# Output projection and routing inside the mixer's block, the front turned by scaled diagonals, token sums in four places

## What is computed

```python
h = rmsnorm(x, g_mix)
q, fg, inp, og, cb, cc, ch, ga, gb = split(h @ w_in)        # 9 slices of 1024 columns
o, s_new = hgrn2_scan(silu(q), (1 - lb) * sigmoid(-fg), inp, logf, s_hg)
o = rmsnorm(o, g_hg_out) * silu(og)
y_a = o @ w_br_a
conv = sum(ext[:, j:j + l] * w_conv[j] for j in range(3))   # ext: cc * ch behind its history
y_b = (cb * conv) @ w_br_b
x = x + (sigmoid(ga) * y_a + sigmoid(gb) * y_b) @ w_out
t = rmsnorm(x, g_ffn)
# top 1 of 4 groups, top 2 of its 8 experts, weights of the two normalised
x = x + hier_moe(t)
x = x + sigmoid(rmsnorm(x, g_ple) @ w_ple_gate) * (p @ w_ple_proj)
return rmsnorm(x, g_final)
```

## Time and profile before

| | |
|---|---|
| median of 3 runs | 1222.99 us (1220.28 to 1223.65) |
| profiled execution | 1231.61 us |
| its span, first to last instruction | 1229.8 us |
| PE busy | 1133.2 us, 92% |
| DVE busy | 641.3 us, 52% |
| POOL, ACT busy | 290.3 and 245.9 us |
| mean granted clock of TensorE | 0.957 |
| moved by DMA | 191.57 MB |

### The profile page before, as it was taken

How to read it: one execution, slowest core, us unless ns; L and a number is a source line. 1 busy time by engine, 2 the same in 40 slices (tenths; PEclk the granted TensorE clock), 3 DMA queues, 4 the chain that set the end, 5 groups by cost and what they waited for, 6 DMA issues and landing times. The chain is left out here.

```text
span 1229.8 us, 15391 instructions
## 1 busy us (share of the span) xinstructions
PE 1133.2 (92%) x5839; PEld 817.8 (67%) x5839; DVE 641.3 (52%) x1279; ACT 245.9 (20%) x446; POOL 290.3 (24%) x242
## 2 busy tenths in 40 slices
PE   4999999999999999899999998898599998887896
PEld 3888888788888877688888884446355554443442
DVE  6356777846477777545535453444234333332655
ACT  3142220104222111341111000111012211112221
POOL 2204221222331113244343440010132221121000
PEclk9999989999999899999999998897699999899998
DMA  6223211321512135222223417303699999997301
GB/s 222 70 71 105 69 35 55 109 86 35 172 39 69 37 108 177 76 70 90 82 69 103 147 49 300 163 35 151 227 386 390 376 383 397 396 399 289 122 34 39
DMA packets 96466, 191.57 MB, mean 156 GB/s; under 512 B 10454, under 2 KB 73766, under 8 KB 84104
## 3 DMA queue, kind: packets, MB, share of 16 engines
q1 hardware_dynamic: 90500, 181.21, 41.0%
q0 software_dynamic: 5440, 8.94, 2.3%
q10 hardware_dynamic: 452, 0.42, 0.1%
HBM read 180.17 MB, written 17.98 MB: 161 GB/s over the span
## 5 line engine op out<-in xcount | busy, mean ns | idle before, releaser
L1093 PE MATMUL ps<-arena,weights 128*128 128x272 f32 x2240 | 535.5, 399 | 6.5 <-DVE arena L765 3.4
L1093 PEld LDWEIGHTS ps<-arena,weights 128*128 128x128 f32 x2240 | 426.6, 192 | 99.5 <-issue 5.1
L583 POOL TENSOR_TENSOR weights<-weights 128x512 f32<-128x512 f32 x160 | 216.7, 1362 | 516.0 <-PE ps L1093 460.1
L1608 PE MATMUL ps<-arena 128*64 128x256 f32 x864 | 108.1, 407 | 16.0 <-DMA arena<-in_w_up 15.9
L1608 PEld LDWEIGHTS ps<-arena 128*64 128x64 f32 x864 | 63.7, 146 | 50.8 <-DMA arena<-in_w_up 17.6
L1686 DVE TENSOR_SCALAR arena<-arena 64x256 f32<-64x256 f32 x32 | 9.1, 286 | 140.5 <-ACT arena L1650 140.5
L1276 PE MATMUL ps<-weights,arena 128*128 128x512 f32 (+1 forms) x160 | 72.0, 653 | 4.2 <-PEq L483 4.2
L627 ACT ACTIVATE arena<-ps 128x272 f32<-128x272 f32 x80 | 31.1, 393 | 219.3 <-PE ps L1093 219.3
L1573 POOL DMA_INDIRECT expert_rows<-arena x32 | 29.3, 914 | 187.1 <-DVE arena L1702 182.1
L771 DVE TENSOR_TENSOR arena<-arena 128x272 f32<-128x272 f32 x40 | 39.8, 996 | 48.7 <-ACT arena L627 48.4
L1863 PE MATMUL ps<-arena 128*128 128x512 f32 (+1 forms) x160 | 63.0, 594 | 1.4 <-DVE arena L1932 1.4
(11 more groups left out here) (244 smaller groups left out, 1184.9 us busy)
## 6 DMA issues: line engine op xcount, KB each, us to landing
weights<-in_w_in SPq DMA_DIRECT2D x36, 1024.0 KB, 5.1
arena<-in_w_gate SPq DMA_DIRECT2D x27, 1024.0 KB, 21.9
arena<-in_w_up SPq DMA_DIRECT2D x27, 1024.0 KB, 28.4
arena<-in_w_down SPq DMA_DIRECT2D x27, 1024.0 KB, 30.5
weights<-in_w_gate SPq DMA_DIRECT2D x5, 1024.0 KB, 24.5
weights<-in_w_up SPq DMA_DIRECT2D x5, 1024.0 KB, 31.7
weights<-in_w_down SPq DMA_DIRECT2D x5, 1024.0 KB, 31.1
arena<-in_x_prompt SPq DMA_DIRECT2D x8, 512.0 KB, 6.2
```

The costliest lines, as they stand in the source:

```text
L583: nc.gpsimd.tensor_tensor(SW[:, i], x, y, op).then_inc(s_ready, 1)
L1093: ins = mm(ps[:, b, 0:HF], w4[:, k, :], x4[:, k, :], start=(k == 0), stop=(k == 3))
L1608: ins = mm(ps[u * UP:u * UP + CAP, 2 + s, 0:DE], xgT[s][:, k, :], w[e % 6][:, k, :], start=(k == 0), stop=(k == KT - 1))
```

## The change

There are four parts. (1) **Front**: x is no longer scaled. DVE multiplies the identity by a tile's root and gets a diagonal (`root_rows`), and PE multiplies the rows of x by the diagonal, which turns and scales at once. The short tile is loaded and squared third instead of fifth, conv history is copied later, POOL's first sums wait for all five diagonals, and the first mixer product waits for tiles 0 to 2. (2) **Token sums**: `cvout` stands after three products of the first gb pair instead of behind the pair, and the four subtractions of T1 stand one behind each og pair. (3) **Projection and routing** move into the mixer's block: the functions `out_sync`, `out_pool`, `out_tensor`, `out_scalar` and `out_vector` are called at the end of each engine's stream, the barrier is gone, and a semaphore `mix_ready`, raised behind each ya pair, stands in its place. (4) **Order** on PE, DVE and ACT in that stage: the projection is cut into quarters (512 columns, four K steps), with the turn, the logits and the rank products between them. The bodies of the moved functions are as before where the diff doesn't show them.

```diff
@@ schedule()
-        ev += [("sq", 2 * p), ("sq", 2 * p + 1), *pair("gb", p), *([] if p else [("cvout", 0), ("T", 1)]), ("stat", 2 * p), ...
-    ev += pairs("og", 0) + pairs("og", 1) + pairs("ga", 0) + pairs("ga", 1) + [("T", 2)] + ...
+        gb = pair("gb", p)
+        ev += [("sq", 2 * p), ("sq", 2 * p + 1), *gb[0:3], *([] if p else [("cvout", 0)]), *gb[3:], ("stat", 2 * p), ...
+    for p in range(4):
+        ev += pair("og", p) + [("T1", p)]
+    ev += pairs("ga", 0) + pairs("ga", 1) + [("T", 2)] + ...
@@ sync
-                for t in range(NT):
+                for t in (0, 1, 4, 2, 3):
...
+                out_sync(sp)
@@ gpsimd
+                pool.wait_ge(d2p, NT)
                 weight_sums(0)
...
+                out_pool(pool)
@@ scalar
-                for x in range(NT):
+                for i, x in enumerate((0, 1, 4, 2, 3)):
...
-                for x in range(2, NT):
-                    n = TOK[x]
-                    nc.scalar.activation(xt[0:n, x, :], xt[0:n, x, :], ACT.Copy, scale=rs[0:n, x:x + 1]).then_inc(a2p, 1)
@@ vector
-                def scaled(t):
+                def root_rows(t):
-                    v.tensor_scalar(xt[0:n, t, :], xt[0:n, t, :], rs[0:n, t:t + 1], None, ALU.mult).then_inc(d2p, 1)
+                    v.tensor_scalar(roots[0:n, t, 0:n], ident[0:n, 0:n], rs[0:n, t:t + 1], None, ALU.mult).then_inc(d2p, 1)
...
+                        v.engine_nop().then_inc(mix_ready, 1)
+                out_vector(dve)
@@ tensor
-                                ins = tr(ps[:, b, k * P:k * P + r], xt[0:r, x, (4 * s + k) * P:(4 * s + k) * P + P], ident[0:r, 0:r])
+                                ins = mm(ps[:, b, k * P:k * P + r], xt[0:r, x, (4 * s + k) * P:(4 * s + k) * P + P], roots[0:r, x, 0:r],
+                                         start=True, stop=True)
...
-                            for t in range(NT):
+                            pe.wait_ge(rows_freed, 2)
+                            for t in range(3):
                                 taken(pe, ("xT", t, 0)), taken(pe, ("xT", t, 1))
@@ out_sync
+            sp.wait_ge(mix_ready, 4)
             for e in (1, 2, 3):
@@ out_pool
+            pool.wait_ge(yb_done, 1)
             nc.gpsimd.memset(xg[0], 0.0).then_inc(xg_zero, 1)
@@ out_tensor
+            def quarter(i, q):
+                t, b, s = ORDER[i], 2 * (i % 2) + q // 2, q // 2
+                if i == 1 and q % 2 == 0:
+                    pe.wait_ge(bank_freed[b], used[b])
+                elif i >= 2 and q == 0:
+                    pe.wait_ge(x1_ready, i - 1)
+                for k in range(4 * (q % 2), 4 * (q % 2) + 4):
+                    if (i, q) == (1, 1) and k == 6:
+                        pe.wait_ge(mix_ready, 4)
+                    ins = mm(ps[:, b, :], m[:, k, tok(t)], W[:, s, k, :], start=(k == 0), stop=(k == KT - 1))
...
+            pe.wait_ge(mix_ready, 3)
+            pe.wait_ge(wo_loaded[0], 16)
+            quarter(1, 0), quarter(1, 1)
+            pe.wait_ge(wo_loaded[1], 16)
+            short_tile()
+            quarter(1, 2)
+            turn_rows(0)
+            quarter(1, 3)
+            logits(0)
+            for i in range(1, NT - 1):
+                quarter(i + 1, 0)
+                if i == 1:
+                    rank(0)
+                turn_rows(i)
+                quarter(i + 1, 1)
+                logits(i)
+                if i == NT - 2:
+                    table(0), total(0)
+                quarter(i + 1, 2)
+                rank(i)
+                if i == NT - 2:
+                    table(1), total(1)
+                quarter(i + 1, 3)
+            table(2), total(2)
+            turn_rows(4)
+            before_rank(4)
+            table(3), total(3)
+            logits(4)
+            own_rank(4)
+            table(4).then_inc(table_sum, 1)
+            total(4).then_inc(rank_ready, 1)
@@ out_vector
-                for i in range(2):
-                    residual(i)
-                    root(i)
-                for i in range(NT):
-                    choose(i)
-                    if 0 < i < NT - 1:
-                        residual(i + 1)
-                    place(i)
-                    if 0 < i < NT - 1:
-                        root(i + 1)
+            dve.wait_ge(tails_out, 32)
+            residual(0)
+            root(0)
+            residual(1)
+            for i in range(NT):
+                choose(i)
+                place(i)
+                if 0 < i < NT - 1:
+                    residual(i + 1)
+                if i + 1 < NT:
+                    root(i + 1)
```

## The result

The changed kernel takes 1195.4 us (median of 4 runs, 1193.8 to 1196.3) against 1223.3 of the kernel before on the same chip: ratio 0.976, 95% interval 0.973 to 0.980. The forecast was 1192, with 1185 to 1206 as its range. Run once more beside three of the experiments it took 1196.6, ratio 0.978 (0.974 to 0.981).

A forecast was written before the change was run, and what follows sets the result against it. The experts' weight stream, started by PE's first products there, was taken as the bound. Terms 3.6 + 9.0 + 4.2 + 3.4 - 1.3 + 5.6 + 8.7 - 2.4 - 0.7 = 30.1, taken as 31: median 1192, range 1185 to 1206.

The forecast's parts named there:

- The bound: Experts' stage: its weight stream sets its length and starts with PE's first products, so gains ahead of 871 us count fully.
- The front: Start of the kernel: first mixer product at 23.2 us instead of 26.8, 3.6 us gained.
- The sums: Token sums T1 in the first gb pair: quarters behind the og pairs are hidden, 9.0 us gained.
- The cover that was named: In og, PE is four banks ahead and DVE idle four of a pair's 13 us; without it at most 9.6.
- The seam: Mixer to projection: 4.2 us of PE idle time and 3.4 of slow clock go; waiting for w_out costs 1.3.
- The routing: Routing stage: copy waits of 5.6 us and slow clock of 8.7 go; rank waits and switches add 2.4.
- The rival of the slow spans that stay: Routing: transposes and 36-column logits remain, so slow spans stay; costs the 8.7, giving 1201; chance 0.20.
- The last tile: End of routing: before_rank(4) and a table ahead of the last logits delay DVE's table; 0.7 us taken from 0.5 to 2.5.
- the timetable: Projection and routing, same durations laid end to end: x1 of the last tile at 830.2 instead of 848.2, 18.0 gained.
- the rivals at 1201 and 1203: Slow spans stay in the routing, 1201, chance 0.20; front and sums give nothing, 1203, chance 0.08.

The follow-up runs named there:

- the block of its own: Changed kernel with output projection and routing in a second block behind a barrier again, the changed order kept within it: 1202.5 us, ratio 0.981 to the kernel before.
- doubled logits: Changed kernel with each tile's logits products done twice, the second time over the first: 1206.6 us, ratio 0.986 to the kernel before.

## Why the prediction was right, and where not

**The bound.** That a gain ahead of the experts is worth its full size holds: the time behind the first expert turn stays within 356.5 and 362.0 us in all kernels, with turns from 828 to 871.

**The front**, 3.6: measured 3.1. The first product was at 23.7 instead of 23.2, and lies between 22.8 and 24.0 in the kernels that have the new front with POOL's wait, so the estimate of 3.6 is within that spread. DVE's root had no stretched instruction (15.56 to 17.70, near the 18.0 with diagonals), and PE's turns of three tiles took 5.74, not 5.2. The wait that POOL was given, which the prediction mentions in half a sentence, carries most of this: without it the diagonals were 2.5 us later, and the first product 4.1.

**The sums**, 9.0: 9.0 against this execution of before, 6.6 against that of the front alone, 8.5 to 9.4 in the kernel with the sums alone. The quarters are hidden. The cover that was named is real: as one block they cost 3.6.

**The seam**, 4.2 + 3.4 - 1.3: the idle time and the slow clock went, and the wait for w_out is 1.83 (1.2 to 1.9 in the other executions). The terms net 6.3, or 5.8 with the wait as it was; the block of its own was 5.4 longer in the trace and 4 to 6 by the ratios. PE idled 1.83, a little over the 1.5 that the prediction allowed. The row names the barrier (PEq), but DVE's last pair was what PE waited for.

**The routing**, 5.6 + 8.7 - 2.4: the waits on the copy and all slow spans went. The price of 2.4 was too high: the rank products waited once ahead of the last tile, 0.31 us. Of the cause that I gave for the 8.7, the first half, "since no wait is left", carried little: with most of the waits put back 1.7 came back. "A wide quarter follows each narrow group" was the half that carried. The rival of the slow spans that stay had its 0.20 for the right reason: the transposes and logits are all still there, and only the wide work between them went against it. Its reason against, that each slow span came behind a wait, was not enough: doubled logits drew two without any.

**The last tile**, -0.7: 0.6, with half of the delay hidden by the loads. The 0.7 was picked from 0.5 to 2.5 and not worked out, so its closeness is partly luck.

**The sum.** Front 3.1, sums 6.6 to 9.0, from the seam to the experts 18.6 against 18.0 of the timetable: 28 to 31, where the medians give 27.9 and I took 31. The interval of the ratio reaches from 25 to 33 us, so the 3 us between are not clear of noise. If they are real, the sums' term is the likeliest place, though no run shows it: the profiled execution of before had the block at 9.0 where another had 6.6, and a view of a single execution can't say so. Two slips stand in the prediction: its terms up to x1 of the last tile add to 18.2 and not 17.8, and 31 is more than both its sum (30.1) and its timetable give. The stated range also takes in the rivals at 1201 and 1203, so that the time lies in it decides nothing between them; the clock of 1.00, the stretch of 28.5 us and the experiments do. The first expert turn came at 834.9 and not near 840, and that is the 5 us of the attention stretch, which is luck of one execution. The attention stretch cost nothing in the forecast, since the gain was taken off the median and not off the profiled time alone.

## What to carry to other kernels

Between narrow products put wide ones, so that no piece of waits and narrow work gets long: that held TensorE's clock at full rate over 80 us here, and putting most of the waits back into that order cost only one slow span of 1.7 us beside their own time. At a seam ask first which engine's last work the next stage needs and start on the tiles that are ready; removing the barrier alone gave 0.4 of 4.2 us. And look at what is queued ahead of the one small transfer that everything waits for: moving two loads of 1 MB behind a gather let it arrive 4.3 us earlier in the trace, where reordering the engine that leads to it gave 0.6.

## What the runs showed of the hardware

VectorE's instructions of three columns took 1.10 to 1.18 us beside GpSimd's additions and 0.16 without, each ending within 0.02 us of one of GpSimd's, and four of 1088 columns 7.17 instead of 5.12. In a stretch that no edit touches the time lost to the granted clock was 1.7 to 11.9 us, from one execution to the next, and the length 439.5 to 446.8; before a stage of one profiled execution is trusted, its slow spans should be counted. A gather of 64 rows behind 7 MB of loads made PE wait 9.4 us, and behind 5 MB 5.5.
